# Differential attention on one core: the second map's weights scaled by ScalarE behind their exponentials

## The reference, cut to what matters

```
s = einsum('bqhcd,bkhcd->bchqk', q, k) * A_QK_DIM ** -0.5      # c = 0, 1: two maps, A_QK_DIM = 64
s = where(q_pos[:, None] >= k_pos[None, :], s, -inf)
p = softmax(s, axis=-1)
a = p[:, 0] - lam * p[:, 1]
out = einsum('bhqk,bkhv->bqhv', a, v)                          # A_V_DIM = 128
```

## Time and profile before

| what | value |
|---|---|
| median of three runs | 1562.22 us (1560.1 to 1564.9) |
| the profiled execution | 1559.63 us, its span 1557.8 us |
| busy PE | 1429.0 us, 92% of the span |
| busy DVE | 864.0 us, 55% |
| busy ACT | 531.4 us, 34% |
| attention, first exponential to last | 850.8 to 1094.6 us of the span |
| L1855, the step that the change moves | 32 instructions, 285 to 487 ns each |

### The profile page before, as it was taken

How to read it: one execution, slowest core, us unless ns; L and a number is a source line. 1 busy time by engine, 2 the same in 40 slices (tenths; PEclk the granted TensorE clock), 3 DMA queues, 4 the chain that set the end, 5 groups by cost and what they waited for, 6 DMA issues and landing times.

```text
span 1557.8 us, 29793 instructions
## 1 busy us (share of the span) xinstructions
PE 1429.0 (92%) x11857; PEld 1345.6 (86%) x11857; DVE 864.0 (55%) x1332; ACT 531.4 (34%) x857; POOL 109.2 (7%) x133
## 2 busy tenths in 40 slices
PE   5999996789999999999999888897699999999997
PEld 4898895569899999999998667675599999999997
DVE  5455448623566666632253888878545666665221
ACT  4333423323422332322234554544243323232110
POOL 0111101201100000000101000010020000000000
PEclk9999998669999999999999999998699999999999
DMA  5444232102222222332225445565022222223320
GB/s 194 83 137 124 58 121 84 44 17 68 82 91 89 91 94 94 106 98 91 72 86 203 166 166 168 181 208 176 5 96 82 95 94 87 91 96 114 113 88 21
DMA packets 44188, 162.57 MB, mean 104 GB/s; under 512 B 5546, under 2 KB 6874, under 8 KB 43866
## 3 DMA queue, kind: packets, MB, share of 16 engines
q1 hardware_dynamic: 38506, 143.77, 28.5%
q0 software_dynamic: 5616, 17.86, 3.5%
HBM read 150.18 MB, written 11.43 MB: 104 GB/s over the span
## 4 chain that ended last, share of the span: by engine, by line
PE 80%; DVE 10%; ACT 4%; issue 4%; DMA 0%; POOL 0%; DVEq 0%; ACTq 0%; POOLq 0%
PE ps L507 56%; PE ps L558 12%; DVE mx L1842 2%; DVE s_sc L1874 1%; PE ps L944 1%; ACT e_att L1289 1%; ACT w_hi L1013 1%; PE ps L868 1%; PE ps L920 1%; PE ps L607 1%; DVE e_att L1855 1%; DVE ps L1839 1%; DVE a_att L1859 1%; PE ps L677 1%; PE ps L789 1%
## 5 line engine op out<-in xcount | busy, mean ns | idle before, releaser
L507 PE MATMUL ps<-h_hi,w_hi 128*128 128x260 f32 x1744 | 496.8, 285 | 9.6 <-DVE h_lo L1398 4.6
L507 PE MATMUL ps<-h_hi,w_lo 128*128 128x260 f32 x1744 | 494.9, 284 | 0.0
L507 PE MATMUL ps<-h_lo,w_hi 128*128 128x260 f32 x1744 | 493.4, 283 | 0.0
L1389 DVE TENSOR_TENSOR w_lo<-raw,w_hi 128x1024 fp32r<-128x1024 f32 (+1 forms) x189 | 244.0, 1291 | 416.6 <-ACT w_hi L1013 416.3
L507 PEld LDWEIGHTS ps<-h_hi,w_hi 128*128 128x128 f32 x1744 | 330.6, 190 | 11.9 <-issue 9.4
L507 PEld LDWEIGHTS ps<-h_lo,w_hi 128*128 128x128 f32 x1744 | 330.4, 189 | 0.2
L507 PEld LDWEIGHTS ps<-h_hi,w_lo 128*128 128x128 f32 x1744 | 330.4, 189 | 0.0
L1013 ACT CAST w_hi<-raw 128x1024 fp32r<-128x1024 f32 (+1 forms) x189 | 208.1, 1101 | 238.8 <-PE ps L507 232.7
L507 PE MATMUL ps<-a_lo,w_hi 128*128 128x260 f32 x704 | 199.0, 283 | 0.0
L507 PE MATMUL ps<-a_hi,w_hi 128*128 128x260 f32 x704 | 198.7, 282 | 0.0
L507 PE MATMUL ps<-a_hi,w_lo 128*128 128x260 f32 x704 | 198.7, 282 | 0.0
(11 more groups left out here) (361 smaller groups left out, 2007.2 us busy)
## 6 DMA issues: line engine op xcount, KB each, us to landing
raw<-in_w_ffn SPq DMA_DIRECT2D x88, 512.0 KB, 3.5
raw<-in_w_down SPq DMA_DIRECT2D x32, 704.0 KB, 4.1
k_pages<-in_cache_k SPq DMA_DIRECT2D x32, 512.0 KB, 3.5
v_pages<-in_cache_v SPq DMA_DIRECT2D x32, 512.0 KB, 6.0
raw<-in_w_rec_in SPq DMA_DIRECT2D x29, 512.0 KB, 5.7
raw<-in_w_att_kv SPq DMA_DIRECT2D x24, 512.0 KB, 3.5
raw<-in_w_rec_out SPq DMA_DIRECT2D x8, 512.0 KB, 3.4
raw<-in_w_att_q SPq DMA_DIRECT2D x8, 512.0 KB, 3.4
```

What stands on the lines that cost most here:

```text
L507: ins = TE.matmul(half(bank, h), w_part[:, buf, w], m_part[:, k_at + k, h * HALF:(h + 1) * HALF], start=start, stop=stop)
L1389: V.tensor_tensor(w_lo[:, n % 2, 0:nk * P], raw[:, n % RAW, 0:nk * P], w_hi[:, n % 2, 0:nk * P].bitcast(F32), ALU.subtract).then_inc(lo_sp ...
```

## The change

The scaling of map 1 goes from DVE to ACT. ACT does it right behind the block's exponentials, in place, as a copy with the row's factor as its scale, after a wait for `rc{k}` from DVE. DVE's L1855 and its step `e{k}` go, and its L1859 waits for the new step `es{k}` of ACT instead. The lists of steps follow.

```diff
-        aA, zA = both("act", "sqq ex0 qb att0 ex1 lrq rq att1 ex2 kr sqk att2 ex3 att3 sqo vr se lrk rk lro ro vt orow")
-        aD, zD = both("dve", "m0 x0 nx0 r0 rc0 e0 a0 m1 x1 nx1 mul0 r1 rc1 e1 a1 red0 m2 x2 nx2 mul1 r2 rc2 e2 a2 red1 "
-                      "m3 x3 nx3 mul2 r3 rc3 e3 a3 red2 mul3 red3 smax dmx qn msv sub ls kn mix lall")
+        aA, zA = both("act", "sqq ex0 es0 qb att0 ex1 es1 lrq rq att1 ex2 es2 kr sqk att2 ex3 es3 att3 sqo vr se lrk rk lro ro vt orow")
+        aD, zD = both("dve", "m0 x0 nx0 r0 rc0 a0 m1 x1 nx1 mul0 r1 rc1 a1 red0 m2 x2 nx2 mul1 r2 rc2 a2 red1 "
+                      "m3 x3 nx3 mul2 r3 rc3 a3 red2 mul3 red3 smax dmx qn msv sub ls kn mix lall")
@@ exps(k), ACT
                     ins.then_inc(sA_.sem, 1)
+                    w = slice(0, (k + 1) * P)
+                    wait(act, sD_, f"rc{k}", r)
+                    S.activation(e_att[:, k % 2, 1, w], e_att[:, k % 2, 1, w], ACT.Copy,
+                                 scale=rs[:, k % 2, 1:2]).then_inc(sA_.sem, 1)
@@ combine(k), DVE
                     V.tensor_tensor(rs[:, b, :], rs[:, b, :], coef[:, :], ALU.mult).then_inc(sD_.sem, 1)
-                    wait(dve, sD_, f"rc{k}", r)
-                    V.tensor_scalar(e_att[:, b, 1, w], e_att[:, b, 1, w], rs[:, b, 1:2], None, ALU.mult).then_inc(sD_.sem, 1)
-                    wait(dve, sD_, f"e{k}", r)
+                    wait(dve, sA_, f"es{k}", r)
                     if k >= 2:
                         wait(dve, sP_, f"t{k - 2}", r)
```

## The result

| | median | runs |
|---|---|---|
| before | 1562.49 us | 20 (1559.15 to 1568.80) |
| changed kernel | 1570.78 us | 20 (1564.08 to 1574.68) |
| ratio | 1.0048 | 95% interval 1.0035 to 1.0061 |

The kernel became slower, by 8.3 us between the medians; 4.8 us had been forecast. The measured time lies in the range of 1562 to 1573 us, but outside the forecast's own range of 1565 to 1569. The profiled execution went from 1559.63 to 1572.03 us, its span from 1557.8 to 1570.3 us.

A forecast was written before the change was run, and what follows sets the result against it. DVE's order was taken to bound blocks 1 to 3 of each attention head; 8 heads x 0.59 us plus 0.12 us made 4.84 us, moving the median from 1562.22 to 1567.1 us, own range 1565 to 1569, 8-in-10 range 1562 to 1573.

The forecast's parts named there:

- The place: Attention, stats(1) to turn(3): DVE's order bounds 15.6 us of a head of about 32; the moved step stands on it.
- The price: ACT's scaling copy, priced from L1024: 723 ns at 512 columns against DVE's 486; blocks 1 to 3 together 0.59 us a head.
- The waits: Between L1853 and L1859: exchanging DVE's own waits for waits across engines costs 0; bounds +0.39 and -0.20 us a head.
- ACT's queue: Work behind the new ACT instruction: L1312 in block 2 starts 1.2 us later, cost 0; as a bound, given no chance.
- The sum: Whole kernel: 8 heads x 0.59 = 4.72 us, plus 0.12 for the last head's block 0, gives 4.84 us.
- All of it reaches the end: Behind turn(3): everything is PE's or moves with it, so the full 4.84 us shows in the kernel's time.
- The rival with more half clock: Turn(3) and parts behind it: more heads at half clock, 1569.4 us with two more, 1572.9 with five; chance 0.20.
- a changed number of heads whose last third runs at half clock: Sign of being wrong: in the new profile, other than two loop heads run turn(3) and its parts at half clock.
- Head 3 idled too and kept the full clock: Argument against more half clock: in head 3 PE also idled before turn(3), which then ran at full clock.
- Part 5: ACT's queue behind the new instruction: PE idles 1.47 us before turn(3), so lateness below that costs 0.
- the longer pause of PE: Before turn(3): the change lengthens PE's idle time by 0.24 us, the reason given for more heads at half clock.

The follow-up runs named there:

- act_twice: Changed kernel with one more ACT copy in place, scale 1.0 by a pointer, ahead of each scaling copy; ratio to before 1.0160, median +23.7 us.
- act_block0: Kernel before with ACT scaling in block 0 only, DVE in blocks 1 to 3; ratio to before 1.0035, run again 1.0024.
- imm_scale: Changed kernel with a constant (1/128) in place of the pointer as the ACT copy's scale; ratio to before 1.0013, median +2.6 us.
- c_before: The kernel before once more, unchanged; ratio to before 1.0010, median +1.1 us.
- warm_before: Kernel before with products of ones that nothing reads added in PE's idle time behind values(1) and values(2), last head also values(0); ratio to before 1.0026.
- c_after: The changed kernel once more, unchanged; ratio to before 1.0046, median +6.0 us.
- fill_blocks12: Against before: ACT scales in blocks 1 and 2 only, DVE doing its reduction of the page's products meanwhile; ratio 0.9919, median -12.9 us.

## Why the prediction was right, and where it was short

- **The place.** Right: DVE's order bounds blocks 1 to 3, and the moved step stands on it. act_twice shows that a us added there is a us of D, 15.6 us and 0.4 in the last head's block 0 for the 15.8 expected; act_block0 shows that block 0 is covered in all heads but the last.
- **The price.** Right to 3 ns: taken from L1024 and not from L1295. imm_scale confirms the reason, the pointer. The table of the Trainium skill (VectorE: DVE Perf Modes, the TRN2 errata) had made 613 ns of the 721 and 327 of DVE's 486; the measured rows decide, and its 6.1 us for the sum is too high: D and block 0 are 4.4 us.
- **The waits.** Right at 0: 0.02 us to each side, and 0.11 us before L1861 with a second wait, as before.
- **ACT's queue.** Right at 0. ACT in order of time in the changed kernel, head 2's block 2 and the last head's block 3, answers to the earlier trace rows:

```profile
937.40 0.61 ACT L1294 ACTIVATE e_att<-e_att,rs 128x384 f32<-128x384 f32 x1 [0.43 <-DVE rs L1857]
937.92 0.57 ACT L1316 COPY kraw<-ps 128x520 f32<-128x520 f32 x1
...
939.82 0.48 ACT L1299 COPY at_t<-ps 128x384 f32<-128x384 f32 x1
...
1111.08 0.58 ACT L1299 COPY at_t<-ps 128x512 f32<-128x512 f32 x1 [0.20 <-PE ps L840]
```

L1316 (L1312 of before) starts 8.82 us behind stats(1) where it had started 7.62 us behind it, 1.20 us later, as forecast. copy_t(2) lost its idle time, as forecast, and still no head's D grew by more than the three instructions' difference; the last head's copy_t(3) kept 0.20 us of room behind the 1.9 us cast.
- **The sum.** 4.84 us forecast, D plus the last head's block 0 is 4.25 + 0.12 = 4.37 us. The missing 0.5 is mostly head 1, where D grew by 0.31 us and not 0.57: in the kernel before its L1855 in block 3 had 0.3 us of idle time in front of it, which the other heads don't have (the earlier trace rows shows it as 0.3 behind L1853) and which the new kernel lacks.
- **"All of it reaches the end", and nothing else.** This is the step that fell short: 8.3 and 6.0 us were measured at the end, and D and block 0 are 4.4 of them. The sum had put everything outside of the moved step at nothing. The first profile has one more head with turn(3) at half clock, P +1.56 us, and the second none more, P +0.2 us over c_before. What is left of the medians, some 2.4 and 1.4 us, cannot be placed by one profile each; both profiles are longer ahead of the attention by more than that (7.4 and 3.7 us). The cause of the rest is open.
- **The rival with more half clock.** It holds in part. 1570.8 us lies where it had put two to five more heads, and the profiles show one and none, so its time fits by luck. The prediction had named "a changed number of heads whose last third runs at half clock" as a sign of being wrong, and the first profile shows it.
- **Its argument.** "Head 3 idled too and kept the full clock" left out what head 3 had done before: its part(1, 0, 3) had run at half clock, which is why its pause was 1.47 us and not 2.84. The 1.47 us that Part 5 takes as ACT's slack is for the same reason the slack of such a head only.
- **Why half clock grows.** The reason given, the longer pause of PE, does not settle where half clock costs: in the kernel before, heads 2 and 4 have the same pause (2.84 and 2.83 us) and turn(3) at half and at full clock, imm_scale has four pauses of 2.8 to 3.0 us and none slow, and warm_before has shorter pauses and four. But the number of heads with half clock anywhere does go with it in the kernels without added products: none at a pause of 1.7 us, 1 at 2.4, 3 to 5 at 2.8 to 3.4, 7 at 3.8, by one or two profiles each.

First profile in all: 4.37 (D and block 0) + 1.56 (P) + 7.42 (before the attention) - 0.83 (behind the last head's L1859) is the whole difference of 12.5 us in the span. Second pair, c_after against c_before: 4.41 + 0.20 + 3.73 - 1.67 (head 0 ahead of D, which c_after ran quicker) - 0.87 is the whole 5.8 us. Only the first term is the same in both.

## What to carry to other kernels

A step on a chain of two engines is not made cheaper by giving it to the engine with less work, when the first has to wait for it: compare the two instructions with their operands (a pointer included), and look for what the first engine could do meanwhile. With that second move, and in blocks 1 and 2 alone, the change paid: -13 us where it had cost 6 to 8, of which -9.1 and +4.25 us are D. And where some of the time hangs on the clock, an edit whose own price is near zero can move the median by 0.2 to 0.35% (act_block0): measure the stretch that the edit touches, look at whether a slow stretch lies where the engine has time to spare, and repeat the kernel before as a kernel of its own.

## What the runs showed of the hardware that was not expected

- A pointer as the scale of an ACT copy costs 90 to 93 ns whatever the columns (721 against 629, 615 against 522, 507 against 417, 402 against 309 ns). The Trainium skill (ScalarE: Activation LUTs, What ACT_TABLE_LOAD costs) gives about 93 ns for each pointer operand; the runs agree.
- Neighbours on DVE without a wait between them overlap: the reduction started 0.09 us after the start of a 0.16 us instruction, and starting 0.10 us earlier in two blocks is 0.20 us a head of what fill_blocks12 gained.
- Filling PE's pauses with 1.02 us products raised the number of heads with turn(3) at half clock (from 2 to 4, and from 3 to 7), in one profile each, and left none with half clock in part(1, 0, 3) (from 3 and 2). The granted clock had its full level (2.4 GHz) during the added product and fell to the half level (1.2 GHz) about turn(3).
- A stretch at half clock costs by where it lies. In part(1, 0, 3) it takes 4.09 us instead of 2.70 and the pause behind it is 1.47 us instead of 2.84, so turn(3) is not later; behind turn(3) it costs 1.14 us.
